# Differential attention inside a decoder trunk: value blocks as the stationary operand, turned probabilities of two query tiles moving, the head norm applied along columns

## What is computed

```python
h = rmsnorm(x, norm_g); proj = h @ w_in                  # 12 groups of channels
# branch B, 4 heads of 128 channels, two 64-wide score maps each:
p = softmax(causal(q_m @ k_m.T))  for m in (0, 1)
a = p[0] - lam * p[1]
o = a @ v                                                 # (rows, 128) for each head
o = rmsnorm(o, subln_g, 1e-5) * (1 - lam_init)            # over the 128 channels of the head
y_b = (o * silu(b_z)) @ w_b_out
# branches A (31-tap conv, layernorm) and C (3-tap conv), then
merged = g0 * y_a + g1 * y_b + g2 * y_c
out = rmsnorm(x + merged @ w_o, final_g)
```

## Time and profile before

| | |
|---|---|
| median of 3 runs | 2308.16 us (2306.93 to 2308.53) |
| the profiled execution, its own time | 2308.06 us |
| its span | 2306.3 us |
| mean granted TensorE clock | 0.998 |
| PE busy | 2278.6 us, 99% |
| PE weight loads busy | 1860.0 us, 81% |
| DVE busy | 1482.0 us, 64% |
| ACT busy | 748.6 us, 32% |
| POOL busy | 258.7 us, 11% |
| DMA queues | 59.6% of 16 engines |

### The profile page before, as it was taken

The page is one execution under the profiler, slowest core; times in us unless marked ns, Lnnn a source line. Parts: engine busy times, 40 slices in busy tenths (PEclk is TensorE's granted clock), DMA queues, the critical chain, the costliest instruction groups (busy, mean ns, idle before and its releaser), DMA issues.

```text
span 2306.3 us, 30415 instructions
## 1 busy us (share of the span) xinstructions
PE 2278.6 (99%) x11248; PEld 1860.0 (81%) x11248; DVE 1482.0 (64%) x3042; ACT 748.6 (32%) x1690; POOL 258.7 (11%) x250
## 2 busy tenths in 40 slices
PE   7999999999999999999999999999999999999998
PEld 6888888878888888888788888888878787888886
DVE  4787867773666665564567667665456666587752
ACT  4333332332333331121344344102135454441021
POOL 3455400100000000010000000001000000000010
PEclk9999999999999999999999999999999999999999
DMA  8877788887555545576644454556664444435555
GB/s 312 275 274 273 269 295 289 289 324 289 187 174 176 182 163 186 198 259 240 239 175 174 163 184 145 183 188 243 253 239 163 152 161 154 155 116 188 191 192 201
DMA packets 90610, 490.84 MB, mean 213 GB/s; under 512 B 9312, under 2 KB 9568, under 8 KB 45408
## 3 DMA queue, kind: packets, MB, share of 16 engines
q1 hardware_dynamic: 90464, 488.90, 59.6%
HBM read 375.61 MB, written 113.25 MB: 212 GB/s over the span
## 4 chain that ended last, share of the span: by engine, by line
PE 95%; DVE 2%; DMA 1%; ACT 1%; issue 1%; SPq 0%; DVEq 0%; ACTq 0%
PE PJ L637 73%; PE SC L696 6%; PE OB L758 5%; PE SC L728 5%; PE TB L737 3%; PE OB L696 1%; PE PJ L696 1%; DMA PX<-x_t 0%; PE TB L764 0%; DMA UC<-x 0%; PE TB L771 0%; DVE ZA L1253 0%; PE SC L637 0%; DVE Wp L1169 0%; PE OB L637 0%
## 5 line engine op out<-in xcount | busy, mean ns | idle before, releaser
L637 PE MATMUL PJ<-hT,Wp 128*128 128x512 f32 x6480 | 1575.6, 395 | 0.5 <-DVE PX L1448 0.5
L637 PEld LDWEIGHTS PJ<-hT,Wp 128*128 128x128 f32 x6480 | 1186.6, 188 | 254.1 <-issue 17.0
L1369 DVE SCALAR_TENSOR_TENSOR ACCS<-UA,col,ACCS 128x512 f32<-128x512 f32 x464 | 358.1, 812 | 0.1
L916 ACT ACTIVATE PX<-SC,negm 128x512 f32<-128x512 f32 (+3 forms) x320 | 196.3, 622 | 93.7 <-DVE negm L1208 73.1
L936 ACT ACTIVATE ZA<-TB 128x512 fp32r<-128x512 f32 (+3 forms) x160 | 85.6, 535 | 394.7 <-PE TB L737 394.6
L1253 DVE TENSOR_TENSOR ZA<-TB,ZA 128x512 fp32r<-128x512 f32 (+3 forms) x160 | 97.6, 610 | 178.4 <-ACT ZA L936 177.6
L1208 DVE TENSOR_REDUCE negm<-SC 128x2 f32<-128x1024 f32 (+3 forms) x160 | 169.2, 1060 | 35.3 <-PE SC L728 33.1
L970 ACT ACTIVATE TG<-PJ,col 128x512 f32<-128x512 f32 x64 | 44.1, 689 | 358.3 <-PE PJ L637 358.3
L758 PEld LDWEIGHTS OB<-VM,ZA 128*128 128x128 f32 x1088 | 145.4, 189 | 11.2
L758 PE MATMUL OB<-VM,ZA 128*128 128x128 f32 (+1 forms) x1088 | 154.1, 281 | 0.0
L696 PE MATMUL SC<-Wp,KM 128*128 128x512 f32 x384 | 121.4, 389 | 0.0
(11 more groups left out here) (172 smaller groups left out, 2016.0 us busy)
## 6 DMA issues: line engine op xcount, KB each, us to landing
Wp<-split_weights SPq DMA_DIRECT2D x264, 1024.0 KB, 4.8
split_weights<-Wp SPq DMA_DIRECT2D x88, 1024.0 KB, 4.9
Wraw<-w_stream SPq DMA_DIRECT2D x88, 512.0 KB, 5.8
KM<-keys SPq DMA_DIRECT2D x24, 512.0 KB, 4.5
VM<-values SPq DMA_DIRECT2D x24, 512.0 KB, 4.2
PX<-x SPq DMA_DIRECT2D x16, 512.0 KB, 6.8
out<-PX SPq DMA_DIRECT2D x16, 512.0 KB, 10.9
keys<-KM SPq DMA_DIRECT2D x12, 512.0 KB, 5.8
```

Source lines behind the costliest of these rows:

```text
L637: mm = pe.matmul(pj(c, r)[:, :], wt, rhs[:, 1 if q == 1 else 0, k, :], start=(n == 0), stop=(n == 3 * ktiles - 1))
L916: a = act.activation(PX[:, t % 2, j, m, 0:w], SC[k][:, m, 0:w], ACT.Exp, bias=negm[:, t % 2, j, m:m + 1], accum_out=lsum[:, t % 2, j, m:m ...
L1369: a = dve.scalar_tensor_tensor(out=acc, in0=src, scalar=col[:, n:n + 1], in1=acc, op0=ALU.mult, op1=ALU.add)
```

## The change

Four things change together.

1. `times_v` works on two query tiles at once (a pair q of tiles 2q and 2q+1). The value blocks are stationary, and the turned probabilities of both tiles move: of two key blocks, high V goes against 512 columns each (high and low half of the probabilities of both tiles), low V against 256 columns each. The output comes out with channels on partitions and query rows along the columns. `turn_a` turns two key blocks of two tiles together, so the units of turning are 144 where there were 160; the steps at which they happen are by a new table (`TURNED`), earlier and denser than before. `PX` is given out as 16 rooms by a table (`ROOMS`) that says for each what must be over before it is written again.
2. The squares for the head norm are now summed over partitions, by a matmul with one column of ones (`sum_squares`, two for each pair, plain fp32), where ACT's accumulator summed them along the row.
3. The scale is now one number for each column. ACT stores the 256 scales of a pair to HBM (4 bytes at a time) from its own DMA queue, waits for that some steps later, and loads them back into all 128 partitions. Of each chunk's last pair the scales are spread by two PE transposes instead (`spread_o`).
4. `turn_o` is gone. `zb_pair` (DVE) multiplies output, scale and gate for 256 columns; ACT copies the gate and the first half of the output aside first (`o_copy`). These buffers lie in `Wraw`, in chunk 0 in three spare rooms of `PX`.

The first waits of a pair's parts, in steps after its last turning: output copied +5, clamped +6, squared +7, summed by PE +10 (chunk 3: +9), scale ready +13 (+12), stored +14 (+13), loaded +18 in chunk 0 and +22, +22, +21 in the others, `zb_pair` +24 in chunk 0 and +30 in the others; the last pair of a chunk has spread +15, `zb_pair` +16, split +17 and +18.

```diff
+TURN_LAG = (12, 11, 10, 10)
+TURN_GAP = (6, 6, 4, 3)
+HI_LAG = (0, 0, 0, -1)
+LO_LAG = (1, 1, 1, 0)
+PV_LAG = (4, 4, 4, 4)
...
-            def times_v(c, h, t, j):
...
-                for b in range(nb):
-                    first, last = j == 0 and b == 0, j == c and b == nb - 1
-                    blk = 4 * j + b
-                    whole = (OB[:, 0:2 * P], AT[:, u % 2, 0, b, :], VM[:, blk, :])
-                    part = (OB[:, 0:P], AT[:, u % 2, 1, b, :], VM[:, blk, 0:P])
-                    for n, (dst, l, r) in enumerate((whole, part) if first else (part, whole)):
-                        mm = pe.matmul(dst, l, r, start=(first and n == 0), stop=(last and n == 1))
-                mm.then_inc(pv_done, 1)
-
-            def turn_o(c, h, t):
-                pe.wait_ge(on_ready, tile_at(c, h, t) + 1)
-                wait(pe, tb_free, TURN["o", c, h, t])
-                pe.transpose(TB[:, 0:P], o1[:, :], identf[:, :]).then_inc(ot_done, 1)
...
+                pe.matmul(O2[:, :, :], hi, AT[:, u % 2, :, a0], start=first, stop=False)
+                pe.matmul(O2[:, :, d1], hi1, AT[:, u % 2, :, a1], start=False, stop=False)
+                pe.matmul(O2[:, 0, d1], lo1, AT[:, u % 2, 0, a1], start=False, stop=False)
+                pe.matmul(O2[:, 0, :], lo, AT[:, u % 2, 0, a0], start=False, stop=last).then_inc(pv_done, 1)
+
+            def sum_squares(c, h, q):
+
+                squares = pair_rooms(c)[1]
+                pe.wait_ge(osq_done, pair_at(c, h, q) + 1)
+                wait(pe, tb_free, TURN["o", c, h, q])
+                for i in range(2):
+                    mm = pe.matmul(TB[:, i:i + 1], squares[:, i * P:(i + 1) * P], onesf[:, 0:1], start=True, stop=True)
+                mm.then_inc(osum_done, 1)
+
+            def spread_o(c, h, q):
+
+                pe.wait_ge(on_ready, pair_at(c, h, q) + 1)
+                wait(pe, tb_free, TURN["s", c])
+                for i in range(2):
+                    mm = pe.transpose(TB[:, i * P:(i + 1) * P], ost[:, 5, i:i + 1].to_broadcast([P, P]), identf[:, :])
+                mm.then_inc(last_spread, 1)
...
+            def o_copy(c, h, q):
+
+                n, r = pair_at(c, h, q), head_group(h, BZ)
+                wait(act, zf_ready, n)
+                act.wait_ge(pj_free[bank(r)], bank_use(c, r) + 1)
+                act.activation(pair_rooms(c)[2], SZB[:, 2 * P * q:2 * P * (q + 1)], ACT.Copy).then_inc(gate_copied, 1)
+                act.wait_ge(pv_done, turned(c, h, q, c, q) + 1)
+                act.activation(pair_rooms(c)[0], O2[:, 0, :], ACT.Copy).then_inc(o_copied, 1)
...
+            def store_scales(c, h, q):
+
+                n = pair_at(c, h, q)
+                act.wait_ge(on_ready, n + 1)
+                act.dma_start(rs[n - c, :, :].rearrange("i p -> p i"), ost[:, 5, :], allow_slow_non_contiguous=True).then_inc(scale_stored, 16)
+
+            def load_scales(c, h, q):
+                n = pair_at(c, h, q)
+                act.wait_ge(scale_stored, 16 * (n - c + 1))
+                act.dma_start(pair_rooms(c)[4], rs[n - c:n - c + 1, :, :].rearrange("o i p -> o (i p)").to_broadcast([P, 2 * P])
+                              ).then_inc(o_spread, 16)
...
-            def o_sum(c, h, t):
...
+            def o_clamp(c, h, q):
+                n = pair_at(c, h, q)
+                dve.wait_ge(o_copied, n + 1)
+                dve.tensor_tensor(pair_rooms(c)[0], pair_rooms(c)[0], O2[:, 1, :], ALU.add).then_inc(ob_free, 1)
...
+            def zb_pair(c, h, q):
...
+                    dve.wait_ge(o_spread, 16 * (n - c + 1))
+                    step(dve.scalar_tensor_tensor(out=ZF, in0=OV, scalar=col[:, COL_SG:COL_SG + 1], in1=OT,
+                                                  op0=ALU.mult, op1=ALU.mult))
+                dve.wait_ge(gate_copied, n + 1)
+                dve.tensor_tensor(ZF, ZF, OG, ALU.mult).then_inc(zf_ready, 1)
```

More of the change, by code:

```diff
@@ L139, in loads_before, with pair_at, turns_in, turns_before @@
     return H * (c - 1 - j) + h
+def pair_at(c, h, q):
+    return 2 * (H * c + h) + q
+def turns_in(c):
+    return 4 * c + 3
+def turns_before(c):
+    return sum(H * turns_in(k) for k in range(c))
+def turned(c, h, q, j, g):
+    return turns_before(c) + h * turns_in(c) + q * (2 * c + 1) + 2 * j + g
+def turned_blocks(c, q, j, g):
+    return [(b, i) for b in (2 * g, 2 * g + 1) for i in range(2) if j < c or b <= 2 * q + i]
 def many_at(c, h, t):
     return 16 * (c - 1) + 4 * h + t
[L147 to L153, removed]
 def wdiff_at(c, h, t):
@@ L287, in tap_table @@
     return table
+ROOMS = [room_table(c) for c in range(NCHUNK)]
 TAPS = [tap_table(c) for c in range(NCHUNK)]
@@ L300, in turn_table, with build @@
                     order["v", c, h] = len(order)
[L301 to L304, removed]
+            for h, q, j, g in turned_at(c, p):
+                order["u", c, h, q, j, g] = len(order)
+            for h, q in pairs_at(c, p - OSUM_LAG[c]):
+                order["o", c, h, q] = len(order)
+            if (H - 1, 1) in pairs_at(c, p - LAST_SPREAD):
+                order["s", c] = len(order)
     return order
 TURN = turn_table()
-LAST_O = [max(TURN["o", c, h, t] for h in range(H) for t in range(NT)) for c in range(NCHUNK)]
-def build(nc, x, x_t, w_stream, cols, final_g, lam_v, out, kd, vd, ws):
+LAST_O = [TURN["s", c] for c in range(NCHUNK)]
+def build(nc, x, x_t, w_stream, cols, final_g, lam_v, out, kd, vd, ws, rs):
     with ExitStack() as ctx:
@@ L437, in build, with room, probs, room_free @@
         dve_step = sem("dve_step")
[L440 to L441 removed]
+        def room(r):
+            return PX[:, r // (2 * KB), r // 2 % KB, r % 2, :]
+        def probs(c, h, t, j, m):
+            return room(ROOMS[c][0][h, t, j, m][0])
+        def room_free(eng, done):
+            if done is not None:
+                eng.wait_ge(comb_done if done[0] == "comb" else t_done, done[1])
+        def pair_rooms(c):
+            if c > 0:
+                return [Wraw[:, k // 4, k % 4 * 2 * P:(k % 4 + 1) * 2 * P] for k in range(5)]
+            return [room(SPARE + k // 2)[:, k % 2 * 2 * P:(k % 2 + 1) * 2 * P] for k in range(5)]
+        O2 = OB[:, :].rearrange("p (a n) -> p a n", a=2)
+        def gate_a(c, m):
+            return room(ROOMS[c][1][m][0])
         def merged(m):
@@ L731, in scores, with turn_a @@
                     mm.then_inc(qk_done, 1)
[L733 to L737, removed]
-                mm.then_inc(t_done, 1)
-            def times_v(c, h, t, j):
[L741 to L745, removed]
+            def turn_a(c, h, q, j, g):
+                pe.wait_ge(comb_done, unit(c, h, 2 * q + 1, j) + 1)
+                wait(pe, tb_free, TURN["u", c, h, q, j, g])
+                for n, (b, i) in enumerate(turned_blocks(c, q, j, g)):
+                    mm = pe.transpose(TB[:, n * P:(n + 1) * P],
+                                      probs(c, h, 2 * q + i, j, 0)[:, b * P:(b + 1) * P], identf[:, :])
+                mm.then_inc(t_done, 1)
@@ L746, in times_v @@
+            def times_v(c, h, q, j, g):
+                n = pair_at(c, h, q)
+                pe.wait_ge(tb_free, TURN["u", c, h, q, j, g] + 1)
+                u = turned(c, h, q, j, g)
+                first, last = j == 0 and g == 0, j == c and g == q
+                if first:
+                    wait(pe, ob_free, n)
+                    if h == 0 and q == 0:
                         wait(pe, fin_freed, 8 * c)
-                    if t == 0:
+                    if q == 0:
                         pe.wait_ge(tb_free, TURN["v", c, h] + 1)
-                if t == 0 and j < c:
+                if q == 0 and g == 0 and j < c:
@@ L872, in value_hi @@
                 act.wait_ge(v_turned, head_at(c, h) + 1)
-                wait(act, pv_done, unit(c, h, 0, 0))
+                wait(act, pv_done, turned(c, h, 0, 0, 0))
                 if h == 0:
```

279 lines of the change are left out of this document (164 added, 115 removed).

## The result

The changed kernel takes 2321.4 us (median of 8 runs, 2317.3 to 2329.4) where the kernel before takes 2308.4 (8 runs, 2306.9 to 2309.2): a ratio of 1.0058, 95% interval 1.0046 to 1.0071. It is slower, by 13 us or 0.6%, where 2287 was forecast. The runs of the kernel after spread over 12 us, those of before over 2. The profiled execution took 2323.4 us with a span of 2321.6.

The account below looks back on a forecast made before the run. PE's own instructions, busy 99% at 2.4 GHz, were taken to bound the kernel. Terms summed to -21.7 us from 2308.1, giving 2286.4; 1 us for small waits made the forecast 2287, range 2281 to 2302.

Parts of the forecast that it names:

- The sum: All PE terms added: -28.6 - 0.5 - 9.0 - 1.4 + 16.8 + 1.0 = -21.7 us from 2308.1, giving 2286.4.
- The turning: Transposes of probabilities: the same 544 blocks in 144 groups for 160, saving about 0.5 us.
- the squares' sums: Two plain fp32 one-column matmuls for each of 32 pairs, 0.525 us a pair, adding 16.8 us.
- a full unit of the value product: `times_v`: two 512- and two 256-column matmuls, 0.697 us where four pairs took 0.92; 112 units save 25.0 us.
- rival C: The 256-column matmul hides its weight load entirely or not at all: 2283 or 2298; far ends 0.08.
- Rival D: Columns alone set the value product's cost: full unit 0.752 before, 0.696 after, sum 2309; chance 0.02.
- Rival A: Scales' trip through HBM holds ACT in chunk 0: mild 2292 to 2303 (0.10), severe 0.06, 2316 at 11.1 us landing.
- the cover behind the load: Chunk 0, time ACT's load may be held before PE waits: 4 us at a head's first pair, 3.4 at its second.
- Against: the payload is 1 KB: The argument against a slow landing of the scales' store in chunk 0: it carries only 1 KB.
- The 7.0 us: Chunk 0: a scales' store landing within about 7.0 us of issue costs PE nothing.
- A's price: Each us of landing beyond 7.0 costs PE 7 us, for seven pairs in chunk 0; 29 us at 11.1.
- Rival B: Shorter covers between combine, turning and product leak 0.5 us for each of 32 pairs, 16 us: 2303; chance 0.12.

Follow-up runs that it names:

- F1: Changed kernel with a pair's scales stored and loaded side by side (128 pieces of 8 bytes), VectorE reading with a step of two: 2286.4 us, ratio 0.9905.
- F4: F1 with 24 small copies on ScalarE ahead of each load of scales in chunk 0: 2328.0 us.
- F5: F1 with 18 small copies on ScalarE ahead of each load of scales in chunk 0: 2309.4 us.
- F3: Changed kernel, but the scales' store writes 256 pieces of 8 bytes (scales beside the powers they were made of): 2286.1 us.
- E1: Changed kernel with all 32 pairs' scales spread by PE transposes, none through HBM: 2322.1 us, ratio 1.0058.
- G1: F1 plus, behind each load of scales, one probe store of constants, in four patterns of 128 pieces: 2300.5 us.
- F2: Changed kernel, but only the first tile's scales of a pair are stored, 128 pieces of 4 bytes, and loaded for both tiles: 2319.6 us.
- E2: Changed kernel, but each load takes the scales of the pair before, so ScalarE waits for no landing except the first pair's: 2296.1 us, ratio 0.9945.
- E4: Changed kernel, but the store writes 128 pieces of 8 bytes instead of 256 of 4, load unchanged: 2286.1 us, ratio 0.9902.
- E3: Changed kernel with chunk 0's load of scales and gating four steps later: 2312.8 us, ratio 1.0018.

## Why the prediction was wrong

**The sum was right in the main.** Its -21.7 us gave 2286.4; chunks 1 to 3 of the kernel after gain 22.1 (the sum put the gain of chunk 0 near zero), and F1, which has the changed instructions and no long wait, takes 2286.4. That they meet to a tenth is luck. The turning saves 0.8 us by the prediction's own prices, not 0.5; the squares' sums were too dear by 1.6; and chunk 0 gains about 2.8 us that no term holds. The kernel before isn't at the full clock throughout, as the prediction read from the earlier trace rows. Behind the gate's wait of 2.3 us it runs at the 1.2 GHz level:

```profile
466.03 4.58 PE L637 MATMUL PJ<-ZC,Wp 128*128 128x512 f32 x12 [2.27 <-ACT TG L970]
```
```profile
466.50:469.70 3.20, 3.20 (x9) 2.45 (x9) 2.52 (x8) 1.37 (x3) 0.55 (x1) 0.50 0.76 300
```

Those twelve matmuls take 4.41 us (to 470.44) where 2.73 is the price, 1.7 more. F1 waits 1.2 us at this gate and keeps the full clock. Two waits in its chunk 0 that the kernel before doesn't have, 1.2 and 0.8 us, take most of that back.

By terms: a full unit of the value product is 0.69 us in the kernel after, from its first start to the next projection, 0.697 forecast:

```profile
2000.47 0.39 PE L870 MATMUL OB<-ZA,VM 128*128 128x512 f32 x1
2000.69 0.39 PE L871 MATMUL OB<-ZA,VM 128*128 128x512 f32 x1
2000.92 0.28 PE L872 MATMUL OB<-ZA,VM 128*128 128x256 f32 x1
2001.04 0.28 PE L873 MATMUL OB<-ZA,VM 128*128 128x256 f32 x1
2001.16 2.00 PE L746 MATMUL PJ<-hT,Wp 128*128 128x512 f32 x8
```
```profile
2025.99 0.61 PE L881 MATMUL TB<-onesf,Wraw 128*128 128x1 f32 x4
2026.46 5.72 PE L746 MATMUL PJ<-hT,Wp 128*128 128x512 f32 x24
```

The 256-column matmuls lie 0.12 apart, the value taken, which settles rival C in its middle. Rival D gives the new unit 0.696 too, so this row can't refute it; D's lower price for the kernel before (0.752 a unit, where the earlier trace rows have 0.92) would have left no gain, and the runs have 22.1 us. What the Trainium skill, TensorE: Matmul & The Clock Gate, section Back-to-back issue gap, gives for an isolated matmul doesn't price this stream: the estimate from it is 0.165 us for a pair of 256 and 128 columns where the earlier trace rows have 0.23. For the new unit the estimate from it, 0.65, is nearer to the 0.69 measured. A pair's sums of squares take 0.47 us in this row; with projections before them they take 0.36 to the next start and 0.48 with what they leave behind, the lower bound, where 0.525 was taken: 1.6 us too dear in all.

**Rival A happened, in its severe form, which had 6 in 100.** Place and queue were right: the waits are at the tanh's bank and at V's `TB`. So was the cover behind the load: F4 and F5 give 4.3 and 3.7 us for its 4.0 and 3.4. The eight steps of the other chunks do hide the same landing. The step that failed is "Against: the payload is 1 KB", and with it the sum's zero for the landing: it was to be within 7.0 us, and in chunk 0 it is 8.5 to 11.2. I took the landing to be like that of the nearest stores, 4.9 us, and set the observed 9.0 and 11.1 aside as the crowded start. The store had no row in the trace before; its bounds were 4.3 and 11.1, and the whole sign of the result hung on where it lay between them. That deserved near even chances, and a range up to 2316 at least. What set it was neither size of payload, nor number of pieces, nor, in the main, traffic: pieces that share 8 bytes.

**The 7.0 us were right for three pairs of seven.** They are the 3.6 us between store and load and the cover behind. The timeline has for each pair of chunk 0 the issue of the store, that of the load, the time between the two (ScalarE goes on at the landing, so this stands for it) and the wait of PE. Store and load are in us from the span's start. The landing less the wait of PE is the landing up to which PE would not have waited:

| head, pair | store | load | landing | PE waited | free up to |
|---|---|---|---|---|---|
| 0, first | 83.47 | 93.35 | 9.88 | 4.41 | 5.47 |
| 0, second | 130.22 | 140.31 | 10.09 | 3.01 | 7.08 |
| 1, first | 161.04 | 170.88 | 9.84 | 4.55 | 5.29 |
| 1, second | 208.18 | 216.74 | 8.56 | 1.48 | 7.08 |
| 2, first | 237.56 | 246.52 | 8.96 | 3.75 | 5.21 |
| 2, second | 283.59 | 292.76 | 9.17 | 2.09 | 7.08 |
| 3, first | 314.00 | 325.22 | 11.22 | 5.14 | 6.08 |

The rows of head 0's second pair:

```profile
130.22 0.38 ACTq L1083 DMA_DIRECT2D output_scales<-ost  x1
...
140.31 0.33 ACTq L1088 DMA_DIRECT2D PX<-output_scales  x1
...
142.23 0.52 PE L846 MATMUL TB<-identf,PX 128*128 128x128 f32 x3 [3.01 <-DVE VM L1462]
```

For the second pairs the prediction's 3.6 + 3.4 = 7.0 came out as 7.08, three times. For the first pairs it had 3.6 + 4.0 = 7.6, and got 5.2 to 6.1. There ScalarE comes to the load at 85.05 (83.99 + 1.06 in the first timeline), 1.6 us after the store of 83.47, where 3.6 were counted; at the second pair above it is 3.4. The store of a first pair is late: VectorE comes to the sums of squares at 81.55, behind its own score work, and the scales are ready at 83.44. So the path to the store had a delay that the sum put at nothing.

The Trainium skill, DMA: Bandwidth & Descriptors, says in the section Rules for kernel authors that a non-contiguous last dimension becomes one descriptor for each element. The trace agrees: the ACT queue's packets fall from 11648 to 8064 when the pieces go from 256 to 128 in each of 28 stores. But F3 has 11648 packets too and is quick. The fixed cost of about 2.0 us in the section Anatomy of one DMA is given there for DMAs that GpSimd issues, and these go out from ScalarE's queue, so the prediction cited a figure for another path. None of these stores met it: the quickest of F1 landed in 2.6 us, the median in 4.0, and the 4-byte ones in 9.1.

**A's price left out the clock.** By the prediction's 7.6 and 7.0 the seven landings make 16.3 us of waits (its 7 us for each us beyond 7.0, at the median of 9.8, makes 20); measured are 24.4, the rest by the late stores. Another 12.6 us came from PE at the 1.2 GHz level behind them. The text named the clock only among things that would make it wrong, without a price. One row to price it was there: the gate's wait of 2.3 us in the kernel before, with 1.7 us of slower matmuls behind it. How long PE waited doesn't alone say whether the clock falls. In the kernel after it stayed at full behind the wait of 3.01 us and was at half behind that of 2.09:

```profile
142.30:145.30 3.00, 3.00 (x15) 2.55 (x16) 1.26 (x3) 1.10 (x3) 2.62 (x1) 1.00 0.58 154
```
```profile
294.70:298.00 3.30, 3.30 (x10) 2.72 (x11) 1.05 (x2) 1.15 (x3) 2.58 (x1) 0.50 0.72 214
```

**Rival B** did not happen: in F1 PE's wait at the turning is 0.6 us in all. E1 shows that it wasn't empty: with 28 more uses of `TB` in the same plan the bank leaks 25 us.

## What to carry to other kernels

When a change puts an engine's in-order queue behind a DMA of a kind the trace doesn't have, the forecast is two-sided until that landing is measured, however small the payload; a probe store like G1's, in a place where nothing waits for it, would show it beforehand. Steps between two operations aren't time between them either: the store came 2 us closer to its load than its steps said, since its input was late. Lay small stores out so that no two pieces share 8 bytes, and let the reading engine undo the order. And when PE is 99% busy, a wait can cost more than its length: what follows it at the slower clock belongs to its price, and the page's 40 slices are too coarse to show it.

## What the runs showed that was not expected

- A store of 128 pieces of 4 bytes lands in 10.6 us when they lie side by side, in 5.7 at every 8 bytes and in 4.3 at every 64 (G1); one of 256 pieces of 8 bytes in 4.3 (F3).
- Beside such stores the others' packets take longer too: the weights' queue, 90464 packets in every kernel, took 63.8% of the engines' span in the kernel after, 63.2% in F2 and 64.0% in E2, but 60.3% in F1 and F3 and 60.6% in E4. That is with spans that differ by no more than 1.7%.
- Behind a wait of PE of 4.4 us, 44 matmuls took 12.45 us for 10.01. With waits up to 2.4 us (F5) chunk 0 kept a mean clock of 0.99, with waits up to 4.5 (F4) 0.97. Behind single waits of 2 to 3 us it fell in some places and not in others.
- The later load of E3 landed in 7.0 us where the earlier one took 4.8, with nothing changed but its place among the weights' transfers; in E2, whose loads go out while a store is on its way, they took 8.9. No run here shows why.
